# Retention by rounded high and low parts, the output gate by tanh, and new step positions in a two-block transformer kernel

## What is computed

```python
def first_block(x, ...):
    xn = rmsnorm(x, norm1_g)
    qa, ka, va, qr, kr, vr, gr, gate_a, gate_b = ...      # columns of xn @ w_in
    o_a = dilated attention, 12 heads of 128 in three groups, mixed by softmax of log-sums
    o_r = retention(qr, kr, vr)                           # 4 heads, dk 256, dv 512
    o_r = head_groupnorm(o_r, g, b) * silu(gr)
    y = sigmoid(gate_a) * (o_a @ w_proj_a) + sigmoid(gate_b) * (o_r @ w_proj_b)
    x = x + y @ w_out
    return x + square(relu(rmsnorm(x) @ w_up)) @ w_down

def second_block(x, ...):
    x = short_conv_layer(x)                               # 1024 -> 4 x 2048 -> 1024
    kvs = shared_kv(x)                                    # six streams, two of them compressed
    o = nsa_attention(q, partial_rope(q), gates, *kvs)    # 16 heads of 64
    x = x + (o * silu(z)) @ w_out                         # z = columns of the same projection as q
    return rmsnorm(x, final_norm)
```

## Time and profile before

| | us |
|---|---|
| median of three runs | 2056.43 |
| profiled execution, reported time | 2055.31 |
| profiled execution, span of its instructions | 2053.3 |
| TensorE busy (its records overlap, their ends are modelled) | 2004.4 |
| DVE busy | 1028.6 |
| ACT busy, of it 45 table loads | 763.4, 57.7 |
| POOL busy | 80.1 |

### The profile page before, as it was taken

The page is one execution under the profiler, slowest core; times in us unless marked ns, Lnnn a source line. Parts: engine busy times, 40 slices in busy tenths (PEclk is TensorE's granted clock), DMA queues, the critical chain, the costliest instruction groups (busy, mean ns, idle before and its releaser), DMA issues.

```text
span 2053.3 us, 22584 instructions
## 1 busy us (share of the span) xinstructions
PE 2004.4 (98%) x9443; PEld 1639.2 (80%) x9443; DVE 1028.6 (50%) x1371; ACT 763.4 (37%) x1209; POOL 80.1 (4%) x132
## 2 busy tenths in 40 slices
PE   7999999999999999999999999999999999999897
PEld 6899987878787888888888888888888778866566
DVE  4444446434343346643344455555454465856675
ACT  4555553332323323442133222222222214366763
POOL 0000000000000000000000000000000000033431
PEclk9999999999999999999999999999999999999999
DMA  5222222222222222233323323332333345210002
GB/s 205 68 77 74 71 83 72 84 86 91 79 94 70 96 89 97 88 103 103 103 83 103 102 88 99 101 100 87 103 103 83 118 123 148 83 42 21 32 21 62
DMA packets 186420, 181.22 MB, mean 88 GB/s; under 512 B 4816, under 2 KB 162896, under 8 KB 186320
## 3 DMA queue, kind: packets, MB, share of 16 engines
q1 hardware_dynamic: 182832, 172.41, 26.9%
q10 hardware_dynamic: 3488, 7.38, 1.3%
HBM read 173.49 MB, written 4.19 MB: 87 GB/s over the span
## 4 chain that ended last, share of the span: by engine, by line
PE 83%; DVE 8%; ACT 6%; issue 2%; DMA 1%; ACTq 0%; SPq 0%; DVEq 0%
PE bank L875 75%; ACT tmp L1130 2%; DVE tl L2109 2%; PE bank L978 2%; DVE rs L2092 1%; PE bank L969 1%; ACT raw L1130 1%; PE bank L1084 1%; ACT wh L1146 1%; PE bank L1110 1%; DVE wl L1596 1%; DVE oT L2118 1%; ACT th L1502 0%; PE bank L885 0%; ACT pb L1130 0%
## 5 line engine op out<-in xcount | busy, mean ns | idle before, releaser
L875 PE MATMUL bank<-xh,wh 128*128 128x512 f32 x1352 | 543.0, 402 | 3.1 <-DVE wl L1596 2.5
L875 PE MATMUL bank<-xh,wl 128*128 128x512 f32 x1352 | 527.4, 390 | 0.0
L875 PE MATMUL bank<-xl,wh 128*128 128x512 f32 x1352 | 527.0, 390 | 0.0
L1596 DVE TENSOR_TENSOR wl<-raw,wh 128x2048 fp32r<-128x2048 f32 (+2 forms) x154 | 342.2, 2225 | 307.4 <-ACT wh L1146 307.1
L1146 ACT CAST wh<-raw 128x2048 fp32r<-128x2048 f32 (+2 forms) x154 | 285.0, 1853 | 384.7 <-PE bank L875 371.3
L875 PEld LDWEIGHTS bank<-xh,wh 128*128 128x128 f32 x1352 | 253.7, 188 | 60.2 <-issue 8.3
L875 PEld LDWEIGHTS bank<-xl,wh 128*128 128x128 f32 x1352 | 253.8, 188 | 54.7 <-issue 4.8
L875 PEld LDWEIGHTS bank<-xh,wl 128*128 128x128 f32 x1352 | 253.4, 187 | 54.6
L875 PE MATMUL bank<-wh,xh 128*128 128x512 f32 x512 | 213.3, 417 | 4.8 <-DVE xl L2136 4.6
L875 PE MATMUL bank<-wl,xh 128*128 128x512 f32 x512 | 201.7, 394 | 0.0
L875 PE MATMUL bank<-wh,xl 128*128 128x512 f32 x512 | 201.7, 394 | 0.0
(11 more groups left out here) (261 smaller groups left out, 2540.5 us busy)
## 6 DMA issues: line engine op xcount, KB each, us to landing
raw<-in_w_in SPq DMA_DIRECT2D x50, 1024.0 KB, 4.9
raw<-in_a_w_in SPq DMA_DIRECT2D x32, 1024.0 KB, 5.6
raw<-in_w_up SPq DMA_DIRECT2D x16, 1024.0 KB, 5.3
raw<-in_w_down SPq DMA_DIRECT2D x16, 1024.0 KB, 5.7
raw<-in_w_proj_b SPq DMA_DIRECT2D x8, 1024.0 KB, 5.0
raw<-in_a_w_out SPq DMA_DIRECT2D x8, 1024.0 KB, 5.6
raw<-in_w_out SPq DMA_DIRECT2D x4, 1024.0 KB, 4.8
raw<-in_w_kv SPq DMA_DIRECT2D x4, 1024.0 KB, 4.9
```

Source lines behind the costliest of these rows:

```text
L875: m = e.matmul(o, p, q, start=k == 0 and n == 0, stop=k == K - 1 and n == 2)
L1596: m = e.tensor_tensor(lo, r, hi, ALU.subtract)
```

## The change

Two things are done and all tables of positions are replaced.

**Retention.** q, k, v and the decayed scores are held as a rounded high part and a low part. ACT casts out of the bank, DVE subtracts; a decayed block is written by DVE (L1804 of the changed kernel), cast by ACT (`decay_parts`), and subtracted by DVE. `decay` and `ret` become three rounded products each. q and k have one set of buffers instead of two, the normed output goes to `vN`, `gated` shares memory with `orl`.

**Gate.** z leaves its bank as tanh(z/2) on ACT, DVE forms (tanh + 1) z, and `gate_o` multiplies by 0.5. The token `silu` is gone.

Besides, `Ab` becomes two buffers and the wait of `cv` for the first fold goes. `ROOT` of the compressed stage goes from 0 to 6.

```diff
-                col((part, h, j), (part, h), j * 128, 8, ("x", 0), "out_a" if j else "out_d")
+                col((part, h, j), (part, h), j * 128, 8, ("x", 0), "out_d")
...
+        extra += [(RET["parts", h, kb], ("decay_parts", h, kb)) for kb in range(4)]
...
-GATED_AT = {(0, 0): 22, (0, 1): 24, (0, 2): 28, (0, 3): 38, (1, 0): 27, (1, 1): 32, (1, 2): 39}
...
+GATED_AT = {(0, 0): 21, (0, 1): 28, (0, 2): 30, (0, 3): 35, (1, 0): 27, (1, 1): 31, (1, 2): 39}
...
+       ("decay", 3, 0): 0, ("ret", 3, 0): 11, ("gated", 3, 0): 35, ("decay", 3, 1): 2, ("ret", 3, 1): 12,
+       ("gated", 3, 1): 36, ("decay", 3, 2): 8, ("ret", 3, 2): 13, ("gated", 3, 2): 36,
+       ("decay", 3, 3): 10, ("ret", 3, 3): 20, ("gated", 3, 3): 65, ("next", 3): 48, ("parts", 0, 0): 6,
+       ("parts", 0, 1): 6, ("parts", 0, 2): 14, ("parts", 0, 3): 16, ("parts", 1, 0): 5,
+       ("parts", 1, 1): 13, ("parts", 1, 2): 14, ("parts", 1, 3): 18, ("parts", 2, 0): 1,
+       ("parts", 2, 1): 5, ("parts", 2, 2): 9, ("parts", 2, 3): 25, ("parts", 3, 0): 0, ("parts", 3, 1): 8,
+       ("parts", 3, 2): 8, ("parts", 3, 3): 13}
-ROOT = {1: 5, 2: 4, 3: 0}
+ROOT = {1: 3, 2: 4, 3: 6}
...
-    Ab = nqu[0][:, :, :].rearrange("p (a b) (c d) -> p a b c d", a=2, c=2)
+    Ab = [t[:, :, :].rearrange("p (a b) (c d) -> p a b c d", a=2, c=2) for t in (nqu[0], nqr[0])]
...
     def qk_slot(part, g, h):
         return qk["qk".index(part) * 4 + h]
 
-    def ret_slot(part, h, j):
-        return qk[(h % 2) * 4 + ("rq", "rk").index(part) * 2 + j]
+    def ret_slot(part, j):
+
+        n = ("rq", "rk").index(part) * 2 + j
+        return rqk[n][:, :], rqk[4 + n][:, :]
+
+    def ret_values(h):
+
+        return rvh[(h + 1) % 2], rvl
+
+    def ret_out(h):
+
+        return vN[h % 2]
+
+    def ret_low(kb):
+
+        return [(a[:, 0, :], a[:, 1, 0:384], b[:, 0:256], b[:, 256:384])[kb] for a, b in ((tmp45, rs), (rsl1, rsl2))]
+
...
         def decay(h, kb):
             n = S - 128 * kb
-            bank = take("aux", ("decay", h, kb), ("rsT", h, kb))
+            bank = take("aux", ("decay", h, kb), ("out_d", "decay", h, kb))
             for j in range(2):
-                w.wait_ge(*told("out_a" if j else "out_d", ("rq", h, j)))
-                w.wait_ge(*told("out_a" if j else "out_d", ("rk", h, j)))
-                kT, qT = ret_slot("rk", h, j), ret_slot("rq", h, j)
-                m = e.matmul(bank[:, 0:n], kT[:, kb * 128:(kb + 1) * 128], qT[:, kb * 128:], start=j == 0, stop=j == 1)
+                w.wait_ge(*told("out_d", ("rq", h, j)))
+                w.wait_ge(*told("out_d", ("rk", h, j)))
+                (kh, kl), (qh, ql) = ret_slot("rk", j), ret_slot("rq", j)
+                for x, (k, q) in enumerate(((kh, qh), (kh, ql), (kl, qh))):
+                    m = e.matmul(bank[:, 0:n], k[:, kb * 128:(kb + 1) * 128], q[:, kb * 128:], start=j == 0 and x == 0,
+                                 stop=j == 1 and x == 2)
             m.then_inc(*tell("decay", h, kb))
 
         def ret(h, qb):
-            rv = vN[(h + 1) % 2]
+            vh, vl = ret_values(h)
             bank = take("aux", ("ret", h, qb), ("oN", h, qb))
-            w.wait_ge(*told("out_a", ("rv", h, 3)))
+            w.wait_ge(*told("out_d", ("rv", h, 3)))
             for kb in range(qb + 1):
-                w.wait_ge(*told("rsT", h, kb))
-                m = e.matmul(bank[:, :], rsT[kb][:, (qb - kb) * 128:(qb - kb + 1) * 128], rv[:, kb, :],
-                             start=kb == 0, stop=kb == qb)
+                w.wait_ge(*told("rs_lo", h, kb))
+                for x, (r, v) in enumerate(((rsh[kb], vh), (rsh[kb], vl), (ret_low(kb)[1], vh))):
+                    m = e.matmul(bank[:, :], r[:, (qb - kb) * 128:(qb - kb + 1) * 128], v[:, kb, :],
+                                 start=kb == 0 and x == 0, stop=kb == qb and x == 2)
             m.then_inc(*tell("ret", h, qb))
...
         def rv(h, b):
             key = ("rv", h, b)
             w.wait_ge(*told("tile", key))
-            w.wait_ge(*(told("values", 7), told("values", 11), told("ret", 0, 3), told("ret", 1, 3))[h])
-            e.copy(vN[(h + 1) % 2][:, b, :], tile_bank(key)[:, :]).then_inc(*tell("out_a", key))
+            if h < 2:
+                w.wait_ge(*told("values", 11 if h else 7))
+            if h:
+                w.wait_ge(*told("oN_turned", h - 1, 3))
+            e.copy(ret_values(h)[0][:, b, :], tile_bank(key)[:, :]).then_inc(*tell("out_a", key))
...
-            w.wait_ge(*(told("scores", 11, 0), told("scores", 11, 0), told("decay", 0, 3), told("decay", 1, 3))[h])
-            e.copy(ret_slot(*key)[:, :], tile_bank(key)[:, :]).then_inc(*tell("out_a", key))
+            w.wait_ge(*(told("decay", h - 1, 3) if h else told("scores", 11, 0)))
+            e.copy(ret_slot(part, j)[0], tile_bank(key)[:, :]).then_inc(*tell("out_a", key))
...
+        def decay_parts(h, kb):
+            w.wait_ge(*told("out_d", "decay", h, kb))
+            if h:
+                w.wait_ge(*told("ret", h - 1, 3))
+            e.copy(rsh[kb][:, :], ret_low(kb)[0]).then_inc(*tell("rs_hi", h, kb))
...
             key = ("nz", f)
             w.wait_ge(*told("tile", key))
             after("kv" if f >= 4 else "conv")
-            e.copy(z_slot(f), tile_bank(key)[:, :]).then_inc(*tell("out_a", key))
-
-        def silu(f):
-            w.wait_ge(*told("out_a", ("nz", f)))
-            act(z_slot(f), z_slot(f), ACT.Silu).then_inc(*tell("silu", f))
+            act(z_slot(f), tile_bank(key)[:, :], ACT.Tanh, scale=0.5).then_inc(*tell("out_a", key))
...
         def ret_qk(part, h, j):
-            if j:
-                return
             key = (part, h, j)
-            w.wait_ge(*told("tile", key))
-            w.wait_ge(*(told("scores", 11, 0), told("scores", 11, 0), told("decay", 0, 3), told("decay", 1, 3))[h])
-            e.tensor_copy(ret_slot(*key)[:, :], tile_bank(key)[:, :]).then_inc(*tell("out_d", key))
+            hi, lo = ret_slot(part, j)
+            w.wait_ge(*told("out_a", key))
+            w.wait_ge(*(told("decay", h - 1, 3) if h else told("scores", 11, 0)))
+            e.tensor_tensor(lo, tile_bank(key)[:, :], hi, ALU.subtract).then_inc(*tell("out_d", key))
+
+        def rv(h, b):
+            key = ("rv", h, b)
+            hi, lo = ret_values(h)
+            w.wait_ge(*told("out_a", key))
+            w.wait_ge(*(told("ret", h - 1, 3) if h else told("scores", 11, 0)))
+            e.tensor_tensor(lo[:, b, :], tile_bank(key)[:, :], hi[:, b, :], ALU.subtract).then_inc(*tell("out_d", key))
...
-            e.tensor_tensor(rsT[kb][:, :], bank_of("aux", ("decay", h, kb))[:, 0:n], dec[:, 0:n], ALU.mult).then_inc(
-                *tell("rsT", h, kb))
+            e.tensor_tensor(ret_low(kb)[0], bank_of("aux", ("decay", h, kb))[:, 0:n], dec[:, 0:n], ALU.mult).then_inc(
+                *tell("out_d", "decay", h, kb))
+
+        def decay_parts(h, kb):
+            w.wait_ge(*told("rs_hi", h, kb))
+            decayed, low = ret_low(kb)
+            e.tensor_tensor(low, decayed, rsh[kb][:, :], ALU.subtract).then_inc(
+                *tell("rs_lo", h, kb))
...
-            if n:
-                w.wait_ge(*told("fold0"))
             for x in range(2):
-                m = e.tensor_tensor(Ab[:, :, p, x, :].rearrange("p a (r n) -> p a n r", r=8),
+                m = e.tensor_tensor(Ab[n][:, :, p, x, :].rearrange("p a (r n) -> p a n r", r=8),
...
+        def nz(f):
+
+            key = ("nz", f)
+            w.wait_ge(*told("out_a", key))
+            stt(z_slot(f), z_slot(f), 1.0, tile_bank(key)[:, :], ALU.add, ALU.mult).then_inc(*tell("out_d", key))
...
-            w.wait_ge(*told("silu", 4 * p + 3))
+            w.wait_ge(*told("out_d", ("nz", 4 * p + 3)))
             w.wait_ge(*told("gathered", p, qb, 1))
             for k, z in ((4, zx), (6, tmp45)) if p else ((0, oT),):
                 n = 2 if p else 4
-                m = e.tensor_tensor(oT[:, k:k + n, c], oT[:, k:k + n, c], z[:, 0 if p else 4:2 if p else 8, c], ALU.mult)
+                m = stt(oT[:, k:k + n, c], oT[:, k:k + n, c], 0.5, z[:, 0 if p else 4:2 if p else 8, c], ALU.mult, ALU.mult)
```

More of the change, by code:

```diff
@@ L384, in make_order @@
     extra += [(KV["x", n], ("x_out", *divmod(n, 2))) for n in range(8)]
-    extra += [(KV["silu"], ("silu", f)) for f in range(4)]
     o += placed(main, extra)
@@ L422, in make_order @@
         o += some(FILL[r][2])
-        if r == SILU_AT:
-            o += [("silu", f) for f in range(4, 8)]
         for G in GATED_AT:
@@ L2157, in end @@
             S_.close(phase, "dve")
[L2159 removed]
+        follow(x_in, w_part, w_piece, x_norm, square, w_, root, norm, q, k_, norm_qk, turn_qk, scores, mix_log, mix_pick, mix, rq, rk, rv, decay, decay_parts, ret, gated_ret, pb, split_oa,
                gb, pa, wo, down, ao, up, c_, u, b_, z, nsa_consts, ck, cv, turn_rs, ks, kw, rope_k, hidden, compressed_k,
[L2161 removed]
+               compressed_v, gates, nq_, rope_q, vsw, cmp_scores, cmp_turn, scores_n, rate, turn_n, gather, nz, gate_o,
```

121 lines of the change are left out of this document (60 added, 61 removed), and 32 rows, old and new, of tables (ATT, FILL).

## The result

The changed kernel takes 2050.62 us (seven runs, 2047.55 to 2051.34), the kernel before 2056.58 beside it on the same chip. The ratio is 0.9967, with an interval of 0.9957 to 0.9977: 6 us less, where 15 were forecast (2041.4), and just above the range's end of 2050. The profiled execution took 2050.88, span 2049.0.

A forecast was written before the change was run, and what follows sets the result against it. It took TensorE as the bound, its chain covering 83% of the span. From the 2056.43 us median, 6.7 - 1.0 + 2.3 + 2.0 + 6.0 - 1.0 = 15.0 us less gave 2041.4, range 2034 to 2050.

The forecast's parts named there:

- Retention, TensorE work: In retention, three rounded products replace each plain f32 product in ret and decay: 6.7 us less, ends 6.7 and 10.5.
- the dear end: In decay, a rounded 128-column product costs 0.22 us, as in f32, not 0.06: 3.5 us more.
- rival A: In retention, narrow rounded products are cheap: TensorE sum 10.5 us instead of 6.7, total 2037.6; chance 0.28.
- New waiting in front of `ret`: In retention, the longer path through DVE and ACT to ret makes TensorE wait 1 us; bounds 0 and 6.
- Rival D: In retention, low halves of 16 decayed blocks reach TensorE 1.3 us late each, costing 21 us: 2061; chance 0.04.
- Compressed stage: At its start, a second buffer removes the folding wait and the sum of squares moves later: 2.3 us less, bounds 0 and 3.1.
- Gate, first place: Before the selected attention's first exp, fewer loads and no silu let exps start earlier: 2.0 us less, bounds -1 and 4.
- Gate, second place: At the first output product, TensorE's 4.00 us wait and the slow clock after it go: 6.0 us less, bounds 2 and 7.5.
- rival B: At the gate, another chain and the gathered output decide, so both gate terms, 8 us, fall away: 2049.4; chance 0.11.
- Placements: New position tables in attention, selected attention and tail change nothing: 0 us, bounds -4 and +4.
- rival C: In attention and tail, new positions cost 6 us: 2047.4; chance 0.12.
- The list of what would show it: Expected trace signs, among them no 4 us gap at the first output product, clock near 1, attention moving under 4 us.

The follow-up runs named there:

- d_narrow: b_ret_fold with 96 more rounded products of 128 columns in retention (first product of each decay of key block 3 done 25 times over); 2054.0 us.
- b_ret_fold: Kernel before with the new retention, two `Ab` buffers and ROOT 6; silu gate and old KV, FILL and GATED_AT stay; 2043.42 us.
- a_ret_only: Kernel before with the new retention alone; silu gate, one `Ab` buffer, old KV, FILL and GATED_AT stay; 2043.38 us.
- c_busy: a_old_late with the first product of tile z 3 done ten times over, same result (9 more products); 2043.25 us.
- a_old_late: Changed kernel with the old KV, FILL and GATED_AT tables, tanh gate kept; 2046.24 us.
- b_tanh_second: a_old_late with tanh only for z 4 to 7, z 0 to 3 gated by copy and silu as before; 2042.87 us.
- b_tanh_first: a_old_late with tanh only for z 0 to 3, z 4 to 7 gated by copy and silu as before; 2043.93 us.
- c_old_att: b_ret_fold with the old ATT table (attention positions) as well; 2042.98 us.
- d_second_busy: b_tanh_second with 5 more products ahead of its boundary wait (first product of tile z 3 done six times over); 2043.18 us.

## Why the prediction was wrong, by its steps

The steps that failed most are those of the last stage. The forecast put the gate at 8 us of gain, less 1 for DVE, and all new positions at 0. At old positions tanh costs 2.8 us instead, and the new positions cost another 4.4. Two smaller errors go the other way: the narrow products were priced at twice what they cost, and the new waiting did not come. That the result still lies near the range's end is luck: by the medians, retention brought some 4 us more than its traces show.

**Retention, TensorE work (6.7 us, ends 6.7 and 10.5).** The step "I take the dear end" for the products of 128 columns failed: 0.11 us instead of 0.22. In my own sum, 24 x 0.11 = 2.6 instead of 5.3, the total is 7.2 + 3.0 - (2.6 - 1.8) = 9.4 (0.8 us dearer than plain f32, not 3.5), and the traces have 9.7 from the end of attention to the end of retention (+1.0 to -8.7). That is rival A in direction, at a price between its end and mine. The other widths were right; of the changed kernel, one triple of `ret` (L1008) takes 349.89 - 349.20 = 0.69 us:

```profile
347.83 0.78 PE L997 MATMUL bank<-rqk 128*128 128x128 f32 x6
348.45 0.44 PE L902 MATMUL bank<-xh,wh 128*128 128x512 f32 x1
...
349.20 0.40 PE L1008 MATMUL bank<-rvh,rsh 128*128 128x512 f32 x1
349.44 0.39 PE L1008 MATMUL bank<-rvl,rsh 128*128 128x512 f32 x1
349.66 0.39 PE L1008 MATMUL bank<-rvh,rsl 128*128 128x512 f32 x1
349.89 0.40 PE L902 MATMUL bank<-xh,wh 128*128 128x512 f32 x1
```

The Trainium skill, TensorE: Matmul & The Clock Gate, section "LDWEIGHTS (loading the stationary operand)", gives a load of P weight columns about P / 1.2 ns: 107 ns for 128 columns. In d_narrow the products of 128 columns and their loads both start 0.11 us apart, so the trace agrees. That the load is what sets this price is argued, not shown; products of 256 columns, at 120 ns, are hardly dearer.

**New waiting in front of `ret` (1.0 us, up to 6).** None: TensorE has no wait between 334 and 724 us. Rival D is out.

**Compressed stage (2.3 us).** Right up to 1723 us, even low: 3.5 us there, of which b_ret_fold has 2.4 over a_ret_only. That it would stay was wrong: b_ret_fold ends where a_ret_only does. It brings TensorE to a boundary that DVE sets.

**Gate, first place (2.0 us, down to -1).** The wrong sign. Two steps failed. The first is that loads and silu make TensorE wait 1.60 us for the exps. c_busy has neither, and waits 1.60 us all the same, since ACT itself now waits for DVE's maxima, at the first exp and at the exps of unit 1, for which TensorE waits ahead of unit 2:

```profile
1796.51 0.37 ACT L1161 ACTIVATE tmp<-bank,rs 128x128 f32<-128x128 f32 x1 [3.48 <-DVE rs L2132]
...
1802.58 0.37 ACT L1161 ACTIVATE tmp<-bank,rs 128x128 f32<-128x128 f32 x1 [3.16 <-DVE rs L2132]
...
1804.23 0.92 PE L1115 MATMUL bank<-ksT,nqr 64*128 64x256 f32 x4 [1.60 <-ACT tmp L1161]
```

b_ret_fold, with loads and silu, has its first exp at 1796.44 and a wait of 1.61. The second is that the eight products "mostly lie beside TensorE work". DVE works nearly without a pause ahead of the boundary (in the kernel before already 18.17 of 20 us from 1760 on, 16.43 from 1780 on), so the products of z delay `pc`, and TensorE's wait grows from 1.1 to 2.3 us. I had looked at ACT alone.

**Gate, second place (6.0 us).** The step that failed is that the whole wait of 4.00 us hangs on loads and silu. At old positions it shrank by 2.0 us: behind silu stood a path of exps, a weight cast, a weight split and the gate's own three operations, with 2.0 us of its own. That is rival B in its outcome and in part in its mechanism, and I gave it 0.11; the gathered output, which B names, had no part in it (in a_old_late it was there by 1824.5). At old positions the second place was worth 0.5 us by itself (b_tanh_second against b_ret_fold), less than the runs can tell, and with tanh at the first place too it cost 2.3 (a_old_late against b_tanh_first). I had booked the slow clock as something that vanishes with its wait; with half clock at the boundary taken away, the full tanh gate is even with silu (c_busy 2043.25, nine products included, b_ret_fold 2043.42).

**Placements (0, within 4).** Attention 0, right; KV and GATED_AT 0, right; FILL cost some 5 us (2050.6 against 2045.2, GATED_AT going with it). That is rival C in the last stage alone. Rivals B and C together are what happened. I had left room for the pair in the chances only; the range's upper end is B alone, and nothing was added up for both: by the measured pieces, retention and compression 12.8 us at 1723 us, the last stage 8.4 us back.

**The list of what would show it.** A TensorE gap of 4 us at the first output product should be gone and the clock near 1: the gap went, the clock is 0.55 from 1904 to 1912. Attention moved by 1.0.

On the clock, the rows first: waits of 1.11 and 0.57 us at 1789 us in b_ret_fold, 1.2 us apart, were followed by a clock of 0.57 over the next four us. The same two waits in a_ret_only (1793.07, 1794.26) left it at 1.00. The Trainium skill, TensorE: Matmul & The Clock Gate, section "A second HAM failure mode: psum-queue depth-cycling", describes this sort: short idle times between groups of products let the clock go back and forth. The trace of b_ret_fold agrees with it; that of a_ret_only shows that the same idle times need not do it.

**What beats both.** Twelve of these kernels have a median at least 3 us under the changed one's. b_tanh_second (2042.87), c_old_att (2042.98), d_second_busy (2043.18), c_busy (2043.25), a_ret_only (2043.38) and b_ret_fold (2043.42) can't be told apart. All have the new retention and the old FILL, and take 0.7% less than the kernel before. b_tanh_first (2043.93), with its bare wait of 2.30 us at the boundary, is hardly behind them.
